# Feed-forward weight blocks whose odd rows lie 128 bytes further modulo 256, in a two-layer decoder step on one core

## The chip, the cores and the metric

The kernel runs on one core of a Trainium2 chip. The metric is the device time of one execution in microseconds, median of several runs; lower is better.

## What is computed

The reference runs two layers over 1,056 tokens (1,024 of a prompt, 32 of eight sampled sequences). Every layer is a mixing part (four token mixers behind one input projection) and a feed-forward part; the change touches only what is here called the channel part, which begins with the output projection:

```python
def finish(x, m, w_o, g_post_mix, g_pre_ffn, g_post_ffn, w_gate, w_up, w_down):
    x = x + rmsnorm(m @ w_o, g_post_mix)
    h = rmsnorm(x, g_pre_ffn)
    f = (jax.nn.silu(h @ w_gate) * (h @ w_up)) @ w_down
    return x + rmsnorm(f, g_post_ffn)
```

D_MODEL is 1024 and D_FF is 2816. Everything is float32 and has to keep float32's accuracy.

## The kernel before

**Three matmuls for one.** The kernel uses the type float32r, which keeps fewer bits. Each weight block and each activation is held as two tensors, a rounded one (`hi`) and the remainder (`lo`). The helper `terms` (its matmuls are recorded at L2199) issues for each product `hi x lo`, `hi x hi` and `lo x hi` (weight first), all into one PSUM bank. Each of the three loads its own 128x128 weights and moves 352 columns.

**Layout of the moving operands.** The T = 1056 tokens are taken in thirds (`th` = 0, 1, 2) of TH = 352. `act_hi` and `act_lo` are [128, 8, 1056] in float32: the row of block k starts 4,224 k bytes behind the start, and the third th 1,408 th bytes further. 4,224 is 16.5 times 256 and 1,408 is 5.5 times 256, so each odd k and th = 1 put the start of the moving operand 128 bytes further modulo 256. The gated activations `a_hi[i]` and `a_lo[i]` lie in places of 4,224 bytes (L2078 to L2086), and in the channel's order one of the pair of an i lies at the one half of 256 bytes and the other at the other half.

**Layout of the weights.** A weight block is 1024 rows by 128 columns, held as [128, 8, 128]: row block k starts 512 k bytes behind the start, so all eight start alike modulo 256. A place (`at_slot`, L2068) has 8,192 bytes, 4,096 for `w_hi` and 4,096 in which `w_raw` lands and `w_lo` replaces it. There are seven places: 0 to 2 go round, 3 to 5 serve the last blocks only, 6 serves block 3. Places 0 to 5 stand alike modulo 256, and alike with k even and th = 0 of the moving operands; place 6 stands 128 bytes off.

**The work of the channel part,** in the order that is written out by hand for TensorE (PE):

- the output projection: for th = 0 eight k's, in each eight output blocks d times three matmuls (24 matmuls on one moving row k); for th = 1 and 2 eight d's, in each eight k's times three. Its weights `wo_hi` and `wo_lo` stand alike modulo 256 for all k and d.
- 60 blocks j (`seq`, L2116) of three thirds, 24 matmuls to a third: 44 gate and up blocks, in parts of 8, 8 and 6 hidden blocks, and after each of the first two parts 8 down blocks, whose moving operands are `a_lo[k]`, `a_hi[k]`, `a_hi[k]`. A gate or up third is eight k's of `act_lo[k]`, `act_hi[k]`, `act_hi[k]`.
- the last six weight blocks (down, `sources[NB + k]`), for th = 0 k by k with eight d's in each, then th = 1 and 2 d by d.

**The supply of weights.** SP (the DMA queue) issues one 512 KB transfer to a block: `load(j)` (L2149, recorded at L2150) waits until the block that used the place is finished, three blocks earlier. ScalarE (ACT) rounds it (`split_w`, recorded at L2413), GpSimd (POOL) takes the remainder (`rest_of_w`, recorded at L2573), and PE waits for POOL's count (`w_lo_done`). VectorE (DVE) and ACT empty the PSUM banks. Nothing but the placement and the transfers of these blocks is changed.

```python
            def load(j):
                sp.dma_start(w_raw[slot(j)][:, 0:sources[j].shape[1], :], sources[j]).then_inc(w_in[slot(j)], 16)
            def terms(b, hi, lo, x_hi, x_lo, first, end):
                for i, (w, x) in enumerate(((hi, x_lo), (hi, x_hi), (lo, x_hi))):
                    ins = pe.matmul(bank(b), w, x, start=first and i == 0, stop=end and i == 2)
                return ins
```

Of the kernel before, what the change touches and what calls it, by code (L numbers as in the profile page):

```python
# [6 lines left out]
ALU = mybir.AluOpType  # L7
ACT = mybir.ActivationFunctionType
AX = mybir.AxisListType
F32 = mybir.dt.float32  # L10
BF16 = mybir.dt.bfloat16
I32 = mybir.dt.int32
F32R = mybir.dt.float32r


P = 128
# [23 lines left out]
KC = D // P  # L40
# [4 lines left out]
T = SEQ + NS  # L45
TH = T // 3
# [25 lines left out]
PAGES_AT = 170720  # L72
EARLY_END = PAGES_AT + 4 * (KIN + 2 * KC * GW + P + NS + P + NS + 4 * len(SLOTS))
# [331 lines left out]
def early_buffers(c, sem):  # L405
# [21 lines left out]
    c.rstd_y, c.rstd_x = (c.nc.alloc_sbuf_tensor_at(n, [P, TH], F32, offset=c.m_at + 24576 + 4 * TH * i) for n, i in (("rstd_y", 3), ("rstd_x", 4)))  # L427
    c.left_part = c.nc.alloc_sbuf_tensor_at("left_part", [P, TH], F32, offset=c.m_at + 24576 + 20 * TH)
# [1609 lines left out]
def channel(c, st):  # L2038
# [8 lines left out]
    def place(name, at, shape, dt=F32):  # L2047
        assert at + 4 * int(np.prod(shape[1:])) <= SBUF_END
        return nc.alloc_sbuf_tensor_at(name + c.tag, shape, dt, offset=at)
# [7 lines left out]
    y_even, y_even2 = place("y_even", c.m_at + 24576, [P, 6, TH]), place("y_even2", at_scr, [P, 2, TH])  # L2057
# [9 lines left out]

    at_slot = [c.m_at + 8192 * s_ for s_ in range(3)] + [rest + 8192 * s_ for s_ in range(3)] + [PAGES_AT]  # L2068
    w_hi = [place(f"w_hi{s_}", a, [P, KC, P], F32R) for s_, a in enumerate(at_slot)]
    w_raw = [place(f"w_raw{s_}", a + 4096, [P, KC, P]) for s_, a in enumerate(at_slot)]  # L2070
    w_lo = [place(f"w_lo{s_}", a + 4096, [P, KC, P], F32R) for s_, a in enumerate(at_slot)]
    sg_first, sg_next = place("silu_first", PAGES_AT + 8 * T, [P, 2, T]), place("silu", c.m_at + 24576, [P, 2, T])
# [11 lines left out]
    sq2, acc2 = place("down_sq", c.m_at + 24576, [P, 2, TH]), place("down_acc", c.m_at + 24576 + 8 * TH, [P, TH])  # L2084
# [61 lines left out]
    with nc.Block() as block:  # L2146
        @block.sync
        def _(sp):
            def load(j):  # L2149
                sp.dma_start(w_raw[slot(j)][:, 0:sources[j].shape[1], :], sources[j]).then_inc(w_in[slot(j)], 16)  # L2150
# [45 lines left out]
        def _(pe):  # L2196
# [58 lines left out]
            for n, (j, th) in enumerate(seq):  # L2255
# [13 lines left out]
                for k in range(K):  # L2269
                    if j == 0:  # L2270
                        pe.wait_ge(h_lo, KC * th + k + 1)
                    if what == "down" and i == 0:
                        pe.wait_ge(a_lo_done, up_nth[chunk(p_, k), th])
                    x_hi, x_lo = (a_hi[k][:, of(th)], a_lo[k][:, of(th)]) if what == "down" else (act_hi[:, k, of(th)], act_lo[:, k, of(th)])
                    ins = terms(unit_bank(n), w_hi[slot(j)][:, k, :], w_lo[slot(j)][:, k, :], x_hi, x_lo, k == 0, k == K - 1)
# [7 lines left out]
            def down(d, k, th):  # L2283
                j = NB + k
                return terms(down_bank(th, d), w_hi[slot(j)][:, d, :], w_lo[slot(j)][:, d, :], a_hi[k][:, of(th)], a_lo[k][:, of(th)], k == 0, k == NL - 1)
# [91 lines left out]
        def _(act):  # L2377
# [32 lines left out]
            def split_w(j):  # L2410
                K = sources[j].shape[1]
                act.wait_ge(w_in[slot(j)], 16 * (loads_before(j) + 1))
                act.activation(w_hi[slot(j)][:, 0:K, :], w_raw[slot(j)][:, 0:K, :], ACT.Copy).then_inc(w_hi_done, 1)  # L2413

# [140 lines left out]
        def _(pool):  # L2555
# [14 lines left out]
            def rest_of_w(j):  # L2570
                K = sources[j].shape[1]
                pool.wait_ge(w_hi_done, j + 1)
                pool.tensor_tensor(w_lo[slot(j)][:, 0:K, :], w_raw[slot(j)][:, 0:K, :], w_hi[slot(j)][:, 0:K, :].bitcast(F32), ALU.subtract).then_inc(w_lo_done, 1)  # L2573

# [208 lines left out]
```

## Time and profile before

| | us |
|---|---|
| median of 3 runs | 3132.66 (3129.66 to 3135.19) |
| the profiled execution's own time | 3102.04 |
| its span, first to last instruction | 3100.3 |
| mean granted TensorE clock | 0.991 |
| PE busy | 3011.1 (97%) |
| POOL busy | 734.4 (24%) |
| ACT busy | 1053.9 (34%) |
| DVE busy | 1434.6 (46%) |

The profile is one execution, and its rows add up to its own span, not to the median. "Busy" of PE is the union of overlapping matmuls: a matmul's own duration (about 320 ns) is twice the distance from its start to the next one's start, so what a matmul costs in a dense stretch is read from starts, or from a stretch's length over its count of matmuls. PEld is the loading of weights, which runs beside the matmuls. The channel part of layer 0 lies from about 680 to 1,530 us, that of layer 1 from about 2,210 us to the end.

### The profile page before, as it was taken

To read this page: it belongs to the slowest core of one execution; us is meant where nothing else is said; L and a number is where in the kernel's file an instruction comes from. 1 tells how busy PE (TensorE), PEld (TensorE's weight loads), DVE (VectorE), ACT (ScalarE), POOL (GpSimd) and SP (SyncE) were. 2 spreads that over 40 slices of the span, in tenths; PEclk is the share of its full clock that TensorE was granted. 3 is DMA by queue.
4 is the path that set the end of the run, shared out by engine and by line. 5 is a ranking of instruction groups with operands and counts; after the bars stand their busy time and mean duration, and the time that the engine had idled before them with its cause. 6 is when DMAs were issued, how large, how long until landed. Compare 5 with 4: busy or idle time off the path is not lost. (4 is left out here: it accounts for less than half of the span.)

```text
span 3100.3 us, 48849 instructions
## 1 busy us (share of the span) xinstructions
PE 3011.1 (97%) x19766; PEld 2644.6 (85%) x19766; DVE 1434.6 (46%) x3278; ACT 1053.9 (34%) x2094; POOL 734.4 (24%) x526
## 2 busy tenths in 40 slices
PE   8999999989999999999999999899999999999998
PEld 6777766669999999999977777665799999999997
DVE  5579675557611111122565887565574111111125
ACT  4376535554311111011333665355542111110112
POOL 3002041324312122243300201313352122121131
PEclk9999999999999999999999999999999999999999
DMA  5120235651211111121321111456411111111131
GB/s 181 37 64 28 70 150 172 226 204 49 71 44 48 48 47 43 48 66 59 113 79 45 47 35 50 181 184 228 169 58 60 48 48 42 48 48 48 41 118 56
DMA packets 254071, 263.54 MB, mean 85 GB/s; under 512 B 24993, under 2 KB 224570, under 8 KB 253850
## 3 DMA queue, kind: packets, MB, share of 16 engines
q1 hardware_dynamic: 233370, 189.11, 19.5%
q0 software_dynamic: 20480, 71.32, 6.6%
q8 instruction: 159, 2.61, 0.3%
q14 instruction: 62, 0.51, 0.1%
HBM read 229.73 MB, written 30.65 MB: 84 GB/s over the span
## 5 line engine op out<-in xcount | busy, mean ns | idle before, releaser
L2199 PE MATMUL ps<-act_lo,w_hi 128*128 128x352 f32 x2112 | 684.2, 324 | 5.0 <-DVE act_lo L2651 3.1
L2199 PE MATMUL ps<-act_hi,w_hi 128*128 128x352 f32 x2112 | 677.9, 321 | 0.0
L2199 PE MATMUL ps<-act_hi,w_lo 128*128 128x352 f32 x2112 | 677.2, 321 | 0.0
L2573 POOL TENSOR_TENSOR w_lo<-w_raw,w_hi 128x1024 fp32r<-128x1024 f32 x132 | 322.0, 2441 | 1022.9 <-ACT w_hi L2413 1022.8
L709 PE MATMUL ps<-w_in_slots,hT 128*128 128x256 f32 (+1 forms) x2048 | 448.5, 375 | 3.4 <-PEq L192 3.4
L709 PEld LDWEIGHTS ps<-w_in_slots,hT 128*128 128x128 f32 x2048 | 374.7, 193 | 58.6 <-issue 12.4
L2199 PEld LDWEIGHTS ps<-act_lo,w_hi 128*128 128x128 f32 x2112 | 396.7, 188 | 10.2 <-issue 5.2
L2664 DVE TENSOR_TENSOR a_raw<-ps,silu 128x352 f32<-128x352 f32 x120 | 63.0, 525 | 728.7 <-PE ps L2199 728.7
L2199 PEld LDWEIGHTS ps<-act_hi,w_hi 128*128 128x128 f32 x2112 | 397.4, 188 | 0.2
L2199 PEld LDWEIGHTS ps<-act_hi,w_lo 128*128 128x128 f32 x2112 | 396.5, 188 | 0.0
L2199 PE MATMUL ps<-a_lo,w_hi 128*128 128x352 f32 x1056 | 344.1, 326 | 0.0
L2199 PE MATMUL ps<-a_hi,w_lo 128*128 128x352 f32 x1056 | 339.9, 322 | 0.0
L2199 PE MATMUL ps<-a_hi,w_hi 128*128 128x352 f32 x1056 | 339.7, 322 | 0.0
L2413 ACT ACTIVATE w_hi<-w_raw 128x1024 fp32r<-128x1024 f32 x132 | 139.7, 1058 | 460.5 <-DMA w_raw<-in_w_down 286.8
L2461 ACT ACTIVATE silu<-ps 128x352 f32<-128x352 f32 x120 | 55.7, 464 | 674.0 <-PE ps L2199 674.0
L712 PE MATMUL ps<-hT,w_in_slots 128*128 128x352 f32 x768 | 229.7, 460 | 0.0
L1157 DVE TENSOR_SCALAR_CACHE_REDUCE mask_c<-score,sel_cand 128x1024 bf16<-128x1024 f32 x248 | 219.2, 939 | 0.4
L712 PEld LDWEIGHTS ps<-hT,w_in_slots 128*128 128x128 f32 x768 | 145.2, 190 | 80.8 <-issue 1.6
L2199 PEld LDWEIGHTS ps<-a_lo,w_hi 128*128 128x128 f32 x1056 | 199.4, 189 | 1.1
L2199 PEld LDWEIGHTS ps<-a_hi,w_hi 128*128 128x128 f32 x1056 | 198.3, 188 | 1.1
L2199 PEld LDWEIGHTS ps<-a_hi,w_lo 128*128 128x128 f32 x1056 | 198.1, 188 | 0.0
L940 ACT ACTIVATE mask_s<-xT,sel_cand 32x2080 bf16<-32x2080 f32 x62 | 125.2, 2020 | 32.9 <-DVE sel_cand L1162 32.6
(368 smaller groups left out, 4255.2 us busy)
## 6 DMA issues: line engine op xcount, KB each, us to landing
w_raw<-in_w_gate SPq DMA_DIRECT2D x44, 512.0 KB, 3.8
w_raw<-in_w_up SPq DMA_DIRECT2D x44, 512.0 KB, 3.8
w_raw<-in_w_down SPq DMA_DIRECT2D x44, 512.0 KB, 3.8
w_in_slots<-in_w_in SPq DMA_DIRECT2D x18, 1024.0 KB, 5.3
xpark<-xT SPq DMA_DIRECT2D x9, 1408.0 KB, 5.7
xT<-xpark SPq DMA_DIRECT2D x6, 1408.0 KB, 15.5
hT<-xpark SPq DMA_DIRECT2D x6, 1408.0 KB, 12.8
wo_raw<-in_w_o SPq DMA_DIRECT2D x16, 512.0 KB, 5.2
```

What stands on the lines that cost most here:

```text
L709: ins = pe.matmul(ps[:m, bank[i], 0:w], hT[:, k, cols(n)], W[:, g % 2, k, 0:w], start=(k == 0), stop=(k == KC - 1))
L712: ins = pe.matmul(ps[:, bank[i], 0:TH], W[:, g % 2, k, n * P:(n + 1) * P], hT[:, k, th * TH:(th + 1) * TH], start=(k == 0), stop=(k == KC ...
L940: act.activation(junk[x], score[x], ACT.Sign, bias=cand[:rows[x], at[x]].bitcast(F32), accum_out=count[:rows[x], at[x]]).then_inc(q["count ...
L1157: return dve.tensor_scalar(junk[x], score[x], value, None, ALU.is_ge, ALU.add, accum_out=acc)
L2199: ins = pe.matmul(bank(b), w, x, start=first and i == 0, stop=end and i == 2)
L2413: act.activation(w_hi[slot(j)][:, 0:K, :], w_raw[slot(j)][:, 0:K, :], ACT.Copy).then_inc(w_hi_done, 1)
L2461: act.activation(sg(f, th), bank(unit_bank(n)), ACT.Silu).then_inc(sg_done, 1)
L2573: pool.tensor_tensor(w_lo[slot(j)][:, 0:K, :], w_raw[slot(j)][:, 0:K, :], w_hi[slot(j)][:, 0:K, :].bitcast(F32), ALU.subtract).then_inc(w_ ...
L2664: dve.tensor_tensor(raw, bank(unit_bank(n)), sg(chunk(p_, i), th), ALU.mult).then_inc(mul, 1)
```

## The change

Each weight tensor becomes [128, 2, 512] with a distance of 4,224 bytes between its two halves: the first holds the row blocks of even k, the second those of odd k (`at_row`). `w_hi` and `w_raw`/`w_lo` are interleaved, 2,048 bytes apart, so a place is 8,320 bytes long instead of 8,192. The start of a row block of odd k is now 128 bytes off that of even k modulo 256. As 8,320 is 32.5 times 256, places 1 and 4 are also shifted by 128 bytes as a whole. `load` issues two transfers of 256 KB, one to a half (even and odd row blocks; for the last six weight blocks even and odd d), and ACT waits for both. ACT and POOL work on [128, 2, 512] instead of [128, 8, 128] with the same 1,024 elements to a partition. What stood behind the three places (`y_even`, `silu`, `down_sq`, `rstd_y` and others) moves by 384 bytes. The order of the matmuls, their counts and their operands are unchanged.

```diff
--- before.py
+++ after.py
@@ -70,6 +70,8 @@
 
 KIN = PAST // 512 * DB * P
 PAGES_AT = 170720
+W_SLOT = 8320
+PAST_SLOTS = 3 * W_SLOT
 EARLY_END = PAGES_AT + 4 * (KIN + 2 * KC * GW + P + NS + P + NS + 4 * len(SLOTS))
 GAINS_AT = 228704
 SBUF_END = 229344
@@ -424,8 +426,8 @@
     c.early_sems = [*c.w_in, *c.ki_sem, c.const_in, c.x_parked, c.x_last_parked]
 
     c.gains = c.nc.alloc_sbuf_tensor_at("gains", [P, 4, KC], F32, offset=GAINS_AT)
-    c.rstd_y, c.rstd_x = (c.nc.alloc_sbuf_tensor_at(n, [P, TH], F32, offset=c.m_at + 24576 + 4 * TH * i) for n, i in (("rstd_y", 3), ("rstd_x", 4)))
-    c.left_part = c.nc.alloc_sbuf_tensor_at("left_part", [P, TH], F32, offset=c.m_at + 24576 + 20 * TH)
+    c.rstd_y, c.rstd_x = (c.nc.alloc_sbuf_tensor_at(n, [P, TH], F32, offset=c.m_at + PAST_SLOTS + 4 * TH * i) for n, i in (("rstd_y", 3), ("rstd_x", 4)))
+    c.left_part = c.nc.alloc_sbuf_tensor_at("left_part", [P, TH], F32, offset=c.m_at + PAST_SLOTS + 20 * TH)
     c.first_root = c.nc.alloc_sbuf_tensor_at("first_root", [P, 3 * P], F32, offset=ROOT_AT)
     c.wo_raw = c.nc.alloc_sbuf_tensor_at("wo_raw", [P, KC, D], F32, offset=c.m_at + 8 * KC * T + 4 * KC * D)
     c.wo_hi = c.nc.alloc_sbuf_tensor_at("wo_hi", [P, KC, D], F32R, offset=c.m_at + 8 * KC * T)
@@ -2054,7 +2056,7 @@
     over = rest + 4 * KC * T
     wo_hi, wo_raw, wo_lo = c.wo_hi, c.wo_raw, c.wo_lo
     at_scr = over + 8 * KC * D
-    y_even, y_even2 = place("y_even", c.m_at + 24576, [P, 6, TH]), place("y_even2", at_scr, [P, 2, TH])
+    y_even, y_even2 = place("y_even", c.m_at + PAST_SLOTS, [P, 6, TH]), place("y_even2", at_scr, [P, 2, TH])
     y_odd = place("y_odd", c.m_at + 13312, [P, KC, TH])
     sq, acc, rstd = place("mix_sq", at_scr + 8 * TH, [P, 2, TH]), place("mix_acc", at_scr + 16 * TH, [P, TH]), place("mix_rstd", at_scr + 20 * TH, [P, TH])
     gains = c.gains
@@ -2065,11 +2067,16 @@
 
 
 
-    at_slot = [c.m_at + 8192 * s_ for s_ in range(3)] + [rest + 8192 * s_ for s_ in range(3)] + [PAGES_AT]
-    w_hi = [place(f"w_hi{s_}", a, [P, KC, P], F32R) for s_, a in enumerate(at_slot)]
-    w_raw = [place(f"w_raw{s_}", a + 4096, [P, KC, P]) for s_, a in enumerate(at_slot)]
-    w_lo = [place(f"w_lo{s_}", a + 4096, [P, KC, P], F32R) for s_, a in enumerate(at_slot)]
-    sg_first, sg_next = place("silu_first", PAGES_AT + 8 * T, [P, 2, T]), place("silu", c.m_at + 24576, [P, 2, T])
+    at_slot = [c.m_at + W_SLOT * s_ for s_ in range(3)] + [rest + W_SLOT * s_ for s_ in range(3)] + [PAGES_AT]
+    w_hi = [place(f"w_hi{s_}", a, [P, 2, T], F32R)[:, :, 0:4 * P] for s_, a in enumerate(at_slot)]
+    w_raw = [place(f"w_raw{s_}", a + 2048, [P, 2, T])[:, :, 0:4 * P] for s_, a in enumerate(at_slot)]
+    w_lo = [place(f"w_lo{s_}", a + 2048, [P, 2, T], F32R)[:, :, 0:4 * P] for s_, a in enumerate(at_slot)]
+    assert W_SLOT >= 4 * T + 4096
+
+    def at_row(w, k):
+        return w[:, k % 2, k // 2 * P:(k // 2 + 1) * P]
+
+    sg_first, sg_next = place("silu_first", PAGES_AT + 8 * T, [P, 2, T]), place("silu", c.m_at + PAST_SLOTS, [P, 2, T])
 
     def sg(f, th):
         return (sg_first if f < 2 else sg_next)[:, f % 2, of(th)]
@@ -2081,7 +2088,7 @@
     a_lo = [place(f"a_lo{i}", at_tile[2 * i + 1], [P, T], F32R) for i in range(KC)]
     a_raw = place("a_raw", over + 12 * T, [P, 2, TH])
     assert over + 12 * T + 8 * TH <= PAGES_AT and max(at_tile) + 4 * T <= GAINS_AT
-    sq2, acc2 = place("down_sq", c.m_at + 24576, [P, 2, TH]), place("down_acc", c.m_at + 24576 + 8 * TH, [P, TH])
+    sq2, acc2 = place("down_sq", c.m_at + PAST_SLOTS, [P, 2, TH]), place("down_acc", c.m_at + PAST_SLOTS + 8 * TH, [P, TH])
     rstd1, rstd2 = c.rstd_y, c.rstd_x
 
 
@@ -2147,7 +2154,8 @@
         @block.sync
         def _(sp):
             def load(j):
-                sp.dma_start(w_raw[slot(j)][:, 0:sources[j].shape[1], :], sources[j]).then_inc(w_in[slot(j)], 16)
+                for b in range(2):
+                    sp.dma_start(w_raw[slot(j)][:, b, :].rearrange("p (a n) -> p a n", a=4), sources[j][:, b::2, :]).then_inc(w_in[slot(j)], 16)
 
             for k in range(2, KC):
                 load_output_rows(c, sp, k)
@@ -2272,7 +2280,7 @@
                     if what == "down" and i == 0:
                         pe.wait_ge(a_lo_done, up_nth[chunk(p_, k), th])
                     x_hi, x_lo = (a_hi[k][:, of(th)], a_lo[k][:, of(th)]) if what == "down" else (act_hi[:, k, of(th)], act_lo[:, k, of(th)])
-                    ins = terms(unit_bank(n), w_hi[slot(j)][:, k, :], w_lo[slot(j)][:, k, :], x_hi, x_lo, k == 0, k == K - 1)
+                    ins = terms(unit_bank(n), at_row(w_hi[slot(j)], k), at_row(w_lo[slot(j)], k), x_hi, x_lo, k == 0, k == K - 1)
                 ins.then_inc(mm, 1)
                 if n == 1:
                     mix_sum_1(2)
@@ -2282,7 +2290,7 @@
 
             def down(d, k, th):
                 j = NB + k
-                return terms(down_bank(th, d), w_hi[slot(j)][:, d, :], w_lo[slot(j)][:, d, :], a_hi[k][:, of(th)], a_lo[k][:, of(th)], k == 0, k == NL - 1)
+                return terms(down_bank(th, d), at_row(w_hi[slot(j)], d), at_row(w_lo[slot(j)], d), a_hi[k][:, of(th)], a_lo[k][:, of(th)], k == 0, k == NL - 1)
 
             def sum_y(th):
                 pe.wait_ge(d_add, (KC - 1) * (th + 1))
@@ -2408,9 +2416,8 @@
                     act.activation(act_hi[:, k, of(th)], y(th, k), ACT.Copy).then_inc(h_hi, 1)
 
             def split_w(j):
-                K = sources[j].shape[1]
-                act.wait_ge(w_in[slot(j)], 16 * (loads_before(j) + 1))
-                act.activation(w_hi[slot(j)][:, 0:K, :], w_raw[slot(j)][:, 0:K, :], ACT.Copy).then_inc(w_hi_done, 1)
+                act.wait_ge(w_in[slot(j)], 32 * (loads_before(j) + 1))
+                act.activation(w_hi[slot(j)], w_raw[slot(j)], ACT.Copy).then_inc(w_hi_done, 1)
 
             for k in range(2, KC):
                 act.wait_ge(wo_in[k], 16)
@@ -2568,9 +2575,8 @@
                     pool.tensor_tensor(y(th, 0), y(th, 0), y(th, k), ALU.add).then_inc(x_add, 1)
 
             def rest_of_w(j):
-                K = sources[j].shape[1]
                 pool.wait_ge(w_hi_done, j + 1)
-                pool.tensor_tensor(w_lo[slot(j)][:, 0:K, :], w_raw[slot(j)][:, 0:K, :], w_hi[slot(j)][:, 0:K, :].bitcast(F32), ALU.subtract).then_inc(w_lo_done, 1)
+                pool.tensor_tensor(w_lo[slot(j)], w_raw[slot(j)], w_hi[slot(j)].bitcast(F32), ALU.subtract).then_inc(w_lo_done, 1)
 
             for k in range(2, KC):
                 pool.wait_ge(wo_hi_done, k - 1)
```

## Rows read from the trace of the kernel before

**Rows 1.** The page: span, busy time, share of the span and instructions of each engine.
```profile
span 3100.3 us, 48849 instructions
...
PE 3011.1 (97%) x19766; PEld 2644.6 (85%) x19766; DVE 1434.6 (46%) x3278; ACT 1053.9 (34%) x2094; POOL 734.4 (24%) x526
```

**Rows 2.** A stretch of layer 1: us, PE busy (matmuls), granted clock, DMA share, GB/s.
```profile
2343.20:3021.40 678.20, 678.20 (x4246) 1.00 0.18 55
```

**Rows 3.** The page's groups of matmuls, all recorded at L2199.
```profile
L2199 PE MATMUL ps<-act_lo,w_hi 128*128 128x352 f32 x2112 | 684.2, 324 | 5.0 <-DVE act_lo L2651 3.1
...
L2199 PE MATMUL ps<-a_lo,w_hi 128*128 128x352 f32 x1056 | 344.1, 326 | 0.0
```

**Rows 4.** Timeline of SP, second half of layer 1: start us, us, engine line op out<-in.
```profile
2566.20 0.37 SPq L2150 DMA_DIRECT2D w_raw<-in_w_gate  x1
...
2589.24 0.37 SPq L2150 DMA_DIRECT2D w_raw<-in_w_gate  x1
2600.69 0.37 SPq L2150 DMA_DIRECT2D w_raw<-in_w_up  x1
...
2657.92 0.37 SPq L2150 DMA_DIRECT2D w_raw<-in_w_gate  x1
```

**Rows 5.** Timeline of PE, output projection of layer 1, first third.
```profile
2234.49 0.32 PE L2199 MATMUL ps<-act_lo,wo_hi 128*128 128x352 f32 x1
...
2238.33 0.32 PE L2199 MATMUL ps<-act_lo,wo_hi 128*128 128x352 f32 x1
...
2242.13 0.32 PE L2199 MATMUL ps<-act_lo,wo_hi 128*128 128x352 f32 x1
```

**Rows 6.** Timeline of PE, output projection: layer 1 second and last third, layer 0 last third.
```profile
2254.21 0.33 PE L2199 MATMUL ps<-act_lo,wo_hi 128*128 128x352 f32 x1
...
2258.07 0.33 PE L2199 MATMUL ps<-act_lo,wo_hi 128*128 128x352 f32 x1
...
2287.22 0.32 PE L2199 MATMUL ps<-act_lo,wo_hi 128*128 128x352 f32 x1
...
2291.03 0.32 PE L2199 MATMUL ps<-act_lo,wo_hi 128*128 128x352 f32 x1
...
754.88 0.32 PE L2199 MATMUL ps<-act_lo,wo_hi 128*128 128x352 f32 x1
...
758.73 0.32 PE L2199 MATMUL ps<-act_lo,wo_hi 128*128 128x352 f32 x1
```

**Rows 7.** Timeline of PE and of its weight load in one gate block.
```profile
2600.02 0.32 PE L2199 MATMUL ps<-act_lo,w_hi 128*128 128x352 f32 x1
...
2600.02 0.19 PEld L2199 LDWEIGHTS ps<-act_hi,w_hi 128*128 128x128 f32 x1
```

**Rows 8.** The answer for the tile w_raw: split, remainder, and transfers to landing.
```profile
L2413 ACT ACTIVATE w_hi<-w_raw x132: 1052/1060/1068, 738.6 to 3009.3; 128x1024 fp32r<-128x1024 f32 x132
L2573 POOL TENSOR_TENSOR w_lo<-w_raw,w_hi x132: 2365/2394/2774, 739.7 to 3013.6; 128x1024 fp32r<-128x1024 f32 x132
...
DMA to landing us min/median/max: 3.3/3.8/6.1
```

**Rows 9.** Timelines of SP, ACT, POOL and PE at the last six blocks of layer 1.
```profile
3001.91 1.75 SPq L2150 DMA_DIRECT2D w_raw<-in_w_down  x4
...
3005.43 1.06 ACT L2413 ACTIVATE w_hi<-w_raw 128x1024 fp32r<-128x1024 f32 x1 [10.46 <-DMA w_raw<-in_w_down]
...
3006.57 9.48 POOL L2573 TENSOR_TENSOR w_lo<-w_raw,w_hi 128x1024 fp32r<-128x1024 f32 x4 [9.11 <-ACT w_hi L2413]
...
3009.39 0.32 PE L2199 MATMUL ps<-a_lo,w_hi 128*128 128x352 f32 x1
```

**Rows 10.** Timelines of SP, ACT and PE where layer 1 starts its second weight block.
```profile
2307.82 0.37 SPq L2150 DMA_DIRECT2D w_raw<-in_w_up  x1
...
2312.91 1.06 ACT L2413 ACTIVATE w_hi<-w_raw 128x1024 fp32r<-128x1024 f32 x1
...
2316.56 0.40 PE L2199 MATMUL ps<-act_lo,w_hi 128*128 128x352 f32 x1 [0.90 <-POOL w_lo L2573]
```

## The prediction, made before the changed kernel was run

> **What bounds the kernel now.** First the page: TensorE is busy for 3011.1 of 3100.3 us, and no other engine for half of the span [rows 1]. Then a stretch of the channel part of layer 1: PE works through 678.20 us without a pause, at a granted clock of 1.00 [rows 2]. There the time is the number of matmuls times the distance from one start to the next, 678.20 / 4246 = 159.7 ns. The change touches the weights of 3 x 2112 matmuls in gate and up blocks and 3 x 1056 in down blocks [rows 3], 6336 + 3168 = 9504 in all. One nanosecond of distance is 9.5 us, or 0.3% of the run. So everything hangs on whether the place of the weights alters the distance.
>
> It does differ between stretches with the same shapes. SP's loads are released by the end of a block, so their distances are PE's pace. The last two down blocks take 2589.24 - 2566.20 = 23.04 us for 144 matmuls, 160.0 ns each. The five gate and up blocks behind them take 2657.92 - 2600.69 = 57.23 us for 360, 159.0 ns each [rows 4]. In the output projection a k of 24 matmuls takes 3.84 us, the next k only 3.80 us, 160.0 against 158.3 ns, and between these two nothing changes but the half of 256 bytes in which the moving row starts [rows 5]. I read from this that the distance depends on how the moving row stands to the weights that are loaded beside it.
>
> Which weights are these? The load for the next matmul starts as the current one starts, both at 2600.02 [rows 7]. So I compare each moving row with the weights of the matmul behind it: "same" (S) where both start in the same half of 256 bytes, "other" (O) where not. The trace doesn't prove this pairing. Block 3 alone has other weights, too few to settle it.
>
> **The change, part by part.**
>
> *Gate and up, 6336 matmuls.* Before, a third runs SSS OOO SSS OOO, as the row's half changes with k and the weights stay: 159.0 ns. After, the weights change with k too. The first two matmuls of a k load weights of the same k, the third those of the next, so it runs SSO SSO, or in th = 1 and in places 1 and 4 OOS OOS. Nothing in the trace has this in a gate block, but the down blocks of before do: their `a_lo` and `a_hi` lie in different halves, and for most of a third they run OSS OSS or SOO SOO, the same cycles. They take 160.0 ns [rows 4]. So I expect 1.0 ns more: 6336 x 1.0 = 6.3 us longer.
>
> *Down, 3168 matmuls.* Their rows change half within k and now the weights change with k: in most places that makes strict alternation, OSOS. No stretch of before shows it. The nearest rows from below are the fast k's of the output projection, 158.3 ns [rows 5]; from above its second third, 24 matmuls in 2258.07 - 2254.21 = 3.86 us, 160.9 ns [rows 6]. That is 1.7 ns less to 0.9 ns more than the 160.0 of now, -5.4 to +2.9 us. I take 159.7, about the middle and the mean of the long stretch [rows 2]: 3168 x -0.3 = -1.0 us.
>
> *Two transfers instead of one.* SP issues 264 for 132. In the middle of the part the supply has slack: a load comes three blocks of 11.45 us ahead, and needs 3.8 us to landing, 1.06 on ACT and 2.39 on POOL [rows 8]. A second issue is 0.37 us. It costs nothing; without this cover each block would pay about half a microsecond. Two places are tight. Where the second block of a layer is loaded, the transfer is issued at 2307.82, and ACT takes it at 2312.91, without a wait for it; landed at 2307.82 + 3.8 = 2311.6 it has 1.3 us left, more than the second issue [rows 10]. At the end, ACT waits for the third of the last six blocks until 3005.43, POOL has its remainder at 3006.57 + 9.48 / 4 = 3008.94, and PE starts on it at 3009.39, only 0.45 us later [rows 9]. There the transfers have run in 4 KB pieces from a contiguous row of `w_down` and are now cut to 512 bytes each; the shortest landing of all, 3.3 us, and the median of 3.8 [rows 8] bound that at 0.5 us, and the second issue adds up to 0.4. So PE waits 0 to 0.5 us at this point of each layer: I take 0.25, twice, 0.5 us. The other three have a pace of 2.37 us on POOL against 3.84 on PE and stay hidden. The copies of `xpark` behind them come some 2 us later, and none is needed before the first third of these blocks ends, some 15 us after PE's start on the third block (four times 24 matmuls).
>
> *ACT and POOL on two runs of 512 elements* instead of one of 1,024: 0, within 0.1 us of either instruction, hidden behind the same 11.45 us, except in the chain just told, where it lies within the 0.25. *The 384 bytes by which `y_even`, `silu` and others move:* 0; they are read by engines that wait for PE.
>
> **Sum:** 6.3 - 1.0 + 0.5 = +5.8 us on the profiled execution's 3102.0. The median of the runs, 3132.7, is 30.6 us above that execution, and I add the difference to it: 3138.5 us. I can't tell under 0.2%, 6.3 us, from no change, so this lies on the border. With the bounds of the down blocks and of the wait, the forecast's own range is +1 to +10 us, 3133 to 3143.
>
> **The rule that speaks against any effect.** The distance does vary with the half, 160.0 against 158.3 ns in neighbouring k's [rows 5]. Against that, the Trainium skill, TensorE: Matmul & The Clock Gate, section "Step by step: what each phase is for", says that the two read ports are independent and that loading the next weights takes no read bandwidth from the running matmul, and its page SBUF — State Buffer, section "Who interferes with whom", that PE never waits on anyone. By that rule the sum would be +0.5 us; by the rows it is +5.8 us. The trace doesn't agree with it in rows 5.
>
> **The rivals.**
>
> 1. *No effect (12%).* The pace would be set by the moving row alone, as the halves of the rows don't change: 3132.7 + 0.5 = 3133 us. For it: in all rows the weights stood still, so I have seen only the row move. Against it: nothing explains then why a row that starts 128 bytes later runs faster. This is also the case in which the change is made but reaches nothing.
>
> 2. *Faster: a steady pairing (25%).* Perhaps the half of the weights that meet a row is that of its own k, because the reads lag behind the starts that the trace shows. Then each gate and up third is now in one relation throughout, all S or all O, as the k's of the output projection are: 158.3 ns in one and 160.0 in the other [rows 5]. Thirds and places share these about evenly, 159.15 on average, which would be no gain. It decides for a gain if both relations, now without any switch of half between k's, settle at the faster figure: 9504 x (159.35 - 158.3) = 10 us less, 3123 us. (159.35 is the mean over both kinds of block, (6336 x 159.0 + 3168 x 160.0) / 9504.) The place is the whole run of blocks; the point from which it shows is a mean under 158.7 ns. If the collisions went altogether, more would come; no row prices that.
>
> 3. *Clearly slower: the bad cycle (13%).* The pace isn't fixed by the sequence of halves alone. The last third of the output projection has the same addresses in both layers, and 24 matmuls take 3.81 us in layer 1 but 3.85 in layer 0, and the second third 3.86 [rows 6]. So there is more than one steady cycle, and gate blocks now are in a good one. If the new pattern locks into that of 160.9 ns: 9504 x 1.55 = 15 us, 3148 us.
>
> **How the numbers follow.** The forecast has 50%, the rivals 12, 25 and 13. Of the forecast, 20 lie within 0.2% and 30 above; with the rivals that makes 0.25 faster, 0.32 the same, 0.43 slower. The predicted time is the forecast's, rounded to 3138. The range of 3117 to 3149 takes in the faster rival with something below it, and the slower one's price; what is left out is mostly a gain larger than any row prices.
>
> **What would show it.** PE's pace by SP's distances: 11.52 us for a gate or up block where it is 11.45 now, and the last down blocks between 11.40 and 11.58 (now 11.52). The third of the last six blocks should have PE waiting for POOL by up to 0.5 us. Loads should land in about 4.2 us, with no wait of PE elsewhere. If gate and up blocks take 11.45 us again, the pairing plays no part; under 11.42, my pairing is the wrong one or the collisions are really gone. A wait of ACT that reaches PE in mid-stream would make the whole account of the transfers wrong.

## The result, and the profile after

| | before | after |
|---|---|---|
| median, 15 runs each | 3133.51 us | 3140.74 us |
| ratio to before, 95% interval | | 1.0027 (1.0020 to 1.0035) |
| the same against before, kernel run again | 3129.95 us | 3142.66 us, 1.0035 (1.0022 to 1.0049) |
| the profiled execution's own time, its span | 3102.04, 3100.3 us | 3140.74, 3138.9 us |
| a gate or up block (5 blocks / 5) | 11.446 us | 11.546 us |
| a gate or up matmul | 159.0 ns | 160.4 ns |
| a down matmul | 160.0 ns | 160.2 ns |

The kernel became slower by 0.27%, 8.5 us by the ratio (6.3 to 11.0). One of the 15 runs of the changed kernel took 6065.44 us and is not counted in the ratio; the medians alone lie 7.2 us apart. The page after, its span and engines, which answer to [rows 1]:

```profile
span 3138.9 us, 48981 instructions
...
PE 3034.1 (97%) x19766; PEld 2655.8 (85%) x19766; DVE 1427.6 (45%) x3278; ACT 1054.4 (34%) x2094; POOL 734.8 (23%) x526
```

The 38.6 us between the two profiled spans are not what the change costs. Before's own median moves from one comparison to the next: 3103 us on the chip that ran most experiments below, 3130 us on another, 3134 us here. The profile of before (3102 us) fits the first, that of after the others. In the first 700 us, which the change doesn't touch, the granted clock was 0.99 in the one and 0.97 in the other. So the two traces may be compared only where PE's pace is read within one stretch at one clock. These are SP's load issues of after in layer 1, in the columns of [rows 4]; `x2` is now a pair of transfers:

```profile
2417.04 0.92 SPq L2158 DMA_DIRECT2D w_raw<-in_w_gate  x2
...
2601.75 0.92 SPq L2158 DMA_DIRECT2D w_raw<-in_w_gate  x2
...
2624.82 0.92 SPq L2158 DMA_DIRECT2D w_raw<-in_w_gate  x2
2636.39 0.92 SPq L2158 DMA_DIRECT2D w_raw<-in_w_up  x2
...
2694.12 0.92 SPq L2158 DMA_DIRECT2D w_raw<-in_w_gate  x2
...
3005.86 0.92 SPq L2158 DMA_DIRECT2D w_raw<-in_w_up  x2
```

And two of before, the issues at the same points of the work as the first and the last of these:

```profile
2382.62 0.37 SPq L2150 DMA_DIRECT2D w_raw<-in_w_gate  x1
...
2967.57 0.37 SPq L2150 DMA_DIRECT2D w_raw<-in_w_up  x1
```

The five gate and up blocks of after in a view by window: us, PE busy (matmuls), granted clock, DMA share, GB/s.

```profile
2636.39:2694.12 57.73, 57.73 (x362) 1.00 0.16 46
```

The clock is 1.00 there, as in [rows 2], and PE never pauses.

Between the first and the last lie 51 blocks of 72 matmuls. Before they take 2967.57 - 2382.62 = 584.95 us, 159.3 ns a matmul; after 3005.86 - 2417.04 = 588.82 us, 160.35 ns. That is 1.05 ns on 9504 matmuls, 10 us. The starts of these matmuls, from the first to the last of each layer, say the same: 783.37 + 776.84 us after, 778.37 + 771.89 before, 9.95 us more. The timing's 8.5 us (6.3 to 11.0) has room for all of it. By kind: the two down blocks take 2624.82 - 2601.75 = 23.07 us (23.04 before), the five gate and up blocks 2694.12 - 2636.39 = 57.73 us (57.23 before). The loss is nearly all in the gate and up blocks.

It isn't spread evenly over them. ACT's first operation after the end of a third is released by PE, so its starts show when the thirds th = 0, 1, 2 of a block end. Two blocks of after, the first in place 1, the second in place 0 (in brackets ACT's wait and who ended it):

```profile
2651.79 0.47 ACT L2468 ACTIVATE silu<-ps 128x352 f32<-128x352 f32 x1 [10.36 <-PE ps L2207]
2655.65 0.47 ACT L2468 ACTIVATE silu<-ps 128x352 f32<-128x352 f32 x1 [3.40 <-PE ps L2207]
2659.48 0.47 ACT L2468 ACTIVATE silu<-ps 128x352 f32<-128x352 f32 x1 [3.36 <-PE ps L2207]
...
2674.91 0.47 ACT L2468 ACTIVATE silu<-ps 128x352 f32<-128x352 f32 x1 [10.47 <-PE ps L2207]
2678.74 0.47 ACT L2468 ACTIVATE silu<-ps 128x352 f32<-128x352 f32 x1 [3.36 <-PE ps L2207]
2682.61 0.47 ACT L2468 ACTIVATE silu<-ps 128x352 f32<-128x352 f32 x1 [3.40 <-PE ps L2207]
```

In place 1 the third th = 1 takes 2655.65 - 2651.79 = 3.86 us and th = 2 takes 3.83; in place 0 it is the other way round, 3.83 and 3.87. Place 1 stands 128 bytes off place 0, and so does th = 1 off th = 2. From the trace's starts in nanoseconds: where the moving row and the weights of its own k start in the same half of 256 bytes, the gaps between starts repeat as 162, 160, 163, 162, 158, 162 ns, each give or take 1, and whole thirds have a mean of 161.0 to 161.1. Where they start in different halves, the gaps settle after up to half of the third at 161, 161, 155 ns, mean 159; with the less regular matmuls ahead of that, whole thirds have 159.4 to 160.0.

The loads, to compare with [rows 8]: operations on the tile `w_raw` with duration in ns min/median/max.

```profile
L2420 ACT ACTIVATE w_hi<-w_raw x132: 1048/1061/1067, 755.4 to 3051.3; 128x1024 fp32r<-128x1024 f32 x132
L2579 POOL TENSOR_TENSOR w_lo<-w_raw,w_hi x132: 2358/2400/2755, 756.5 to 3053.6; 128x1024 fp32r<-128x1024 f32 x132
...
DMA to landing us min/median/max: 3.9/4.4/5.5
```

ACT and POOL work as long as before, and a pair of transfers holds SP for 0.92 us where it was 0.37. The landing, 4.4 us at the median against 3.8 [rows 8], may not be put down to the change: only 8 of the 264 transfers have one in this trace, and on the chip of 3130 us the kernel's single transfers land later, too. The same line of two kernels below, first the two transfers alone on the chip of 3103 us, then the shift of 128 bytes, with one transfer to a block, on that of 3130 us:

```profile
DMA to landing us min/median/max: 2.9/3.3/5.6
...
DMA to landing us min/median/max: 4.5/5.3/6.1
```

On the first chip both transfers of a pair are there 3.86 us after the first is issued (median of 131 pairs), where one of 512 KB takes 3.81. The 5.3 us rest on four transfers.

The third of the last six blocks of layer 1, to compare with [rows 9]: ACT's split of it, POOL's remainder, PE's last matmul before it and first on it, and the weight load of that one.

```profile
3044.65 1.06 ACT L2420 ACTIVATE w_hi<-w_raw 128x1024 fp32r<-128x1024 f32 x1 [10.56 <-DMA w_raw<-in_w_down]
...
3045.79 2.40 POOL L2579 TENSOR_TENSOR w_lo<-w_raw,w_hi 128x1024 fp32r<-128x1024 f32 x1 [9.23 <-ACT w_hi L2420]
...
3047.85 0.32 PE L2207 MATMUL ps<-a_hi,w_lo 128*128 128x352 f32 x1
3048.24 0.43 PE L2207 MATMUL ps<-a_lo,w_hi 128*128 128x352 f32 x1
...
3048.24 0.19 PEld L2207 LDWEIGHTS ps<-a_lo,w_hi 128*128 128x128 f32 x1 [0.36 <-POOL w_lo L2579]
```

ACT gets the block at 3044.65, POOL ends at 3045.79 + 2.40 = 3048.19, and the weight load behind it has waited 0.36 us for that. PE starts 0.39 us after the matmul before, where 0.16 is the pace, and this matmul lasts 0.43 instead of 0.32: together 0.34 us are lost.

Where the second block begins, to compare with [rows 10]: SP's issue, ACT's split, PE's start.

```profile
2341.92 0.93 SPq L2158 DMA_DIRECT2D w_raw<-in_w_up  x2
...
2347.00 1.06 ACT L2420 ACTIVATE w_hi<-w_raw 128x1024 fp32r<-128x1024 f32 x1
...
2350.64 0.40 PE L2207 MATMUL ps<-act_lo,w_hi 128*128 128x352 f32 x1 [0.81 <-POOL w_lo L2579]
```

ACT takes the tile without a wait for its transfers, and PE's wait for POOL is 0.81 us (0.90 before).

### The profile page after: what moved, and what is told of

The parts are those of the page before. It is cut to its first block and busy times, and to the rows that moved or that the text cites. A ratio compares the mean times of both kernels' runs of the same rounds, so it can differ in the third digit from the quotient of the medians.

```text
span 3138.9 us, 48981 instructions
## 1 busy us (share of the span) xinstructions
PE 3034.1 (97%) x19766; PEld 2655.8 (85%) x19766; DVE 1427.6 (45%) x3278; ACT 1054.4 (34%) x2094; POOL 734.8 (23%) x526
```

## The experiments

Eleven kernels were run, each timed against the kernel before on the same chip. In the stretches compared, the granted clock was 1.00 in every trace. Pace is read as above, from SP's issues around the same five gate and up blocks (360 matmuls). "Own k" means that a moving row is compared with the weights of its own k, "next matmul" with those of the matmul behind it, as the forecast had it.

### The two transfers alone

The kernel before with its layout, each load cut into even and odd row blocks.

```diff
             def load(j):
-                sp.dma_start(w_raw[slot(j)][:, 0:sources[j].shape[1], :], sources[j]).then_inc(w_in[slot(j)], 16)
+                for h in range(2):
+                    sp.dma_start(w_raw[slot(j)][:, h::2, :], sources[j][:, h::2, :]).then_inc(w_in[slot(j)], 16)
...
-                act.wait_ge(w_in[slot(j)], 16 * (loads_before(j) + 1))
+                act.wait_ge(w_in[slot(j)], 32 * (loads_before(j) + 1))
```

> The old placement (all row blocks alike modulo 256), but each block loaded in two transfers of 256 KB. Theory (the pace follows the placement, the transfers cost only at the end of a layer): gate and up blocks 11.45 us apart and down blocks 11.52 us apart as before; PE waits for POOL's remainder of the third of the last six blocks, 0.2 to 0.4 us in each layer; in total 0.4 to 0.8 us over the kernel before, which timing can't tell from nothing (ratio 1.000). Rival (the 4.4 us that each layer's blocks gained come from the transfers, through later weights or busier queues): blocks at 11.53 us again, ratio near 1.0025.

Measured: 3105.77 against 3103.02 us, ratio 1.0004 (0.9995 to 1.0013). SP's issues around the five blocks, and the weight load of PE at the third of the last six blocks:

```profile
2605.28 0.92 SPq L2151 DMA_DIRECT2D w_raw<-in_w_up  x2
...
2662.51 0.92 SPq L2151 DMA_DIRECT2D w_raw<-in_w_gate  x2
...
3014.43 0.19 PEld L2200 LDWEIGHTS ps<-a_lo,w_hi 128*128 128x128 f32 x1 [0.57 <-POOL w_lo L2574]
```

The five blocks take 57.23 us, exactly before's. The one thing that moves is PE's wait, 0.57 us here and 0.36 in layer 0, which the kernel before doesn't have. The transfers cost some 0.5 us a layer at that place and nothing elsewhere. The converse, the new layout with one transfer to a block, was not tried.

### The longer places alone

The blocks as before, but with 8,320 bytes from place to place.

```diff
-    at_slot = [c.m_at + 8192 * s_ for s_ in range(3)] + [rest + 8192 * s_ for s_ in range(3)] + [PAGES_AT]
+    at_slot = [c.m_at + 8320 * s_ for s_ in range(3)] + [rest + 8320 * s_ for s_ in range(3)] + [PAGES_AT]
```

(and 24,960 for 24,576 where `y_even` and what follows begin)

> The old blocks and one transfer each, only with places of 8,320 bytes, so that places 1 and 4 as a whole stand 128 bytes off. Theory (row block against row block decides, and a third still runs through k's in the same relation and k's in the other one by turns): gate and up 11.45 us, ratio 1.000. Rival (the length of the places, or what moved behind them, slows the kernel): 11.5 us or more in all blocks, ratio 1.002 or more.

Measured: 3106.58 against 3103.02 us, 1.0007 (0.9998 to 1.0016).

```profile
2607.28 0.37 SPq L2150 DMA_DIRECT2D w_raw<-in_w_up  x1
...
2664.55 0.37 SPq L2150 DMA_DIRECT2D w_raw<-in_w_gate  x1
```

57.27 us for the five blocks. A shift of whole places by 128 bytes, and the 384 bytes by which `y_even` and others move, cost nothing that the timing can tell. The trace has a little: over both layers, from the first to the last matmul of the weight blocks, 1.75 us more than before, 1.0 of them in gate and up thirds, where the mean is 159.14 ns for 158.99. With the 1.0 us that the same count gives for the two transfers alone, some 7 of the 9.95 us remain. They go with the new layout of a block: the weights of odd k lie 128 bytes off those of even k, and `w_hi` and `w_lo` are interleaved. No kernel had the second without the first.

### All places alike, in either half

The changed kernel with places of 8,448 bytes (33 times 256), so that all stand as place 0 does; and the same with all of them 128 bytes further, as place 1.

```diff
-W_SLOT = 8320
+W_SLOT = 8448
```
```diff
-    at_slot = [c.m_at + W_SLOT * s_ for s_ in range(3)] + [rest + W_SLOT * s_ for s_ in range(3)] + [PAGES_AT]
+    at_slot = [c.m_at + 128 + W_SLOT * s_ for s_ in range(3)] + [rest + 128 + W_SLOT * s_ for s_ in range(3)] + [PAGES_AT]
```

> The changed kernel with places of 8,448 bytes, 33 times 256, so that all places but the seventh stand alike. In the changed kernel's trace a gate or up third in which moving row and weights of the same k start in the same half of 256 bytes runs at 161.0 ns per matmul, and one in which they start in different halves settles at 159.0. Theory (that relation decides): now thirds 0 and 2 run at 161.0 and third 1 at 159.0 in every place, 2 of 3 slow instead of 5 of 9: mean 160.5 to 160.6 instead of 160.4, 11.56 us to a block, about 1 us more than the changed kernel, ratio 1.003. Rival (each place's own stretch of memory or the changes between places cost the time): the places all run like place 0 or better and the ratio falls to 1.001.

> As places_alike, with places 0 to 5 all moved by 128 bytes. Theory: the roles change, thirds 0 and 2 settle at 159.0 ns and third 1 runs at 161.0, 1 of 3 slow: mean 159.9 ns with the first matmuls of a third, 11.51 us to a block, some 4 us less than places_alike, ratio 1.0015 to 1.002. It decides against any theory in which the distance between blocks of odd and even k costs the time by itself: by that one this kernel is as slow as places_alike, ratio 1.003.

Measured: 3110.93 us, 1.0026 (1.0015 to 1.0036), and 3108.76 us, 1.0019 (1.0010 to 1.0028), both against 3103.02. First the places alike: SP around the five blocks, and the ends of the thirds of one block that lies in place 1.

```profile
2606.34 0.92 SPq L2158 DMA_DIRECT2D w_raw<-in_w_up  x2
...
2664.14 0.92 SPq L2158 DMA_DIRECT2D w_raw<-in_w_gate  x2
...
2621.77 0.46 ACT L2468 ACTIVATE silu<-ps 128x352 f32<-128x352 f32 x1 [10.38 <-PE ps L2207]
2625.60 0.46 ACT L2468 ACTIVATE silu<-ps 128x352 f32<-128x352 f32 x1 [3.37 <-PE ps L2207]
2629.46 0.46 ACT L2468 ACTIVATE silu<-ps 128x352 f32<-128x352 f32 x1 [3.40 <-PE ps L2207]
```

Then the places 128 bytes further, the same block:

```profile
2605.71 0.92 SPq L2158 DMA_DIRECT2D w_raw<-in_w_up  x2
...
2663.24 0.92 SPq L2158 DMA_DIRECT2D w_raw<-in_w_gate  x2
...
2621.03 0.46 ACT L2468 ACTIVATE silu<-ps 128x352 f32<-128x352 f32 x1 [10.39 <-PE ps L2207]
2624.90 0.46 ACT L2468 ACTIVATE silu<-ps 128x352 f32<-128x352 f32 x1 [3.40 <-PE ps L2207]
2628.72 0.47 ACT L2468 ACTIVATE silu<-ps 128x352 f32<-128x352 f32 x1 [3.37 <-PE ps L2207]
```

Alike, th = 1 takes 3.83 us and th = 2 takes 3.86; in the changed kernel the block in this place had 3.86 and 3.83. Shifted back by 128 bytes it has 3.87 and 3.82 again. Which thirds are slow therefore follows the half of the place and of th together, by own k: same half 161.0 to 161.3 ns over whole thirds, other half 158.8 to 160.0. With two slow thirds of three the five blocks take 57.80 us, with one 57.53, and the changed kernel, which mixes the places, lies between with 57.73. The timing alone doesn't part the two, as their intervals overlap; by the starts of the matmuls the second is 4.4 us quicker, as expected. By "next matmul" a shift by 128 bytes turns SSO into OOS, and all thirds would have kept one pace.

### The remainder alone 128 bytes further

The kernel before with `w_hi` where it was and `w_raw`/`w_lo` 128 bytes further, in places of 8,448 bytes.

```diff
-    w_raw = [place(f"w_raw{s_}", a + 4096, [P, KC, P]) for s_, a in enumerate(at_slot)]
-    w_lo = [place(f"w_lo{s_}", a + 4096, [P, KC, P], F32R) for s_, a in enumerate(at_slot)]
+    w_raw = [place(f"w_raw{s_}", a + 4224, [P, KC, P]) for s_, a in enumerate(at_slot)]
+    w_lo = [place(f"w_lo{s_}", a + 4224, [P, KC, P], F32R) for s_, a in enumerate(at_slot)]
```

> The old blocks and one transfer each, in places of 8,448 bytes that all stand alike, but w_lo (and w_raw) 128 bytes off w_hi modulo 256. So the weights change half twice in every k, at the third matmul and back. The runs so far: a third in one relation all through runs at 161.0 (same half) or 159.0 ns (other half) where weights and rows change half with every k, at 160.0 or 158.3 in the output projection where neither does, and at 159.0 where only the rows do. Theory A (relation of row and own weights, plus about 0.85 ns a matmul, 2.5 ns a change, for a change of half of the weights): mean 159.15 + 2 x 0.85 = 160.8 ns in gate and up, 11.58 us to a block, ratio 1.003 to 1.004. Theory B (the relation alone, half of the matmuls in either): 159.1 to 159.3, 11.46 us, ratio 1.000 to 1.001.

Measured: 3109.17 against 3103.28 us, 1.0017 (1.0008 to 1.0027).

```profile
2604.46 0.37 SPq L2150 DMA_DIRECT2D w_raw<-in_w_up  x1
...
2661.92 0.37 SPq L2150 DMA_DIRECT2D w_raw<-in_w_gate  x1
```

57.46 us, 159.6 ns, with thirds of 158.9, 159.7 and 160.3 ns; down blocks 160.8. This meets neither of the figures that were set against each other. What the moving rows of a k meet within three matmuls matters, but no rule that I had gives the size.

### The whole weights shifted by 64, 32, 96 and 128 bytes

The kernel before, all seven places shifted by one constant; nothing else but the start of `y_even` and what follows.

```diff
-    at_slot = [c.m_at + 8192 * s_ for s_ in range(3)] + [rest + 8192 * s_ for s_ in range(3)] + [PAGES_AT]
+    at_slot = [c.m_at + 64 + 8192 * s_ for s_ in range(3)] + [rest + 64 + 8192 * s_ for s_ in range(3)] + [PAGES_AT + 64]
```

> The old kernel with all weight places 64 bytes further. If the memory is divided into two halves of 256 bytes, a distance of 64 (or 192) bytes is neither the same nor the other half: gate and up between 158.3 and 161.0 ns, about 159.5, ratio 1.000 to 1.003, and third 1 as third 0. If the division is finer than 128 bytes and collisions are what the distance contains above the shortest ones seen, 155 ns, moving all weights by 64 bytes may take them out of the way: 157 ns or less, 11.3 us to a block, ratio 0.995 or less. If only 128 matters and not where in it a block starts, 159.0 and ratio 1.000.

> The same with 32 bytes. As for 64: about 159 to 160 ns and a ratio within 0.2% of 1 if the halves of 256 bytes are what counts; another value than with 64, in either direction and by more than 0.5 ns, if a finer division does.

> The old kernel with all weight places 96 bytes further; 0, 64 and 32 bytes gave 159.0, 160.2 and 162.0 ns in gate and up. If only the distance of the two starts counts, whichever is ahead, 96 is as far from 128 as 32 is from 0 and costs as much: 162 ns, ratio 1.007. If who is ahead counts, another value: between 159 and 161, ratio 1.000 to 1.004. A gain (below 158.5 ns) would beat both kernels; I give that 1 in 5.

> The old kernel with all weight places 128 bytes further. In a gate or up third same and other half only trade places: 159.0 ns, 11.45 us, ratio within 0.1% of 1. If the half in which weights lie counts by itself: another pace in all thirds, 160 ns or 158.

| shift | median, before's | ratio (95%) | gate, up ns | down ns |
|---|---|---|---|---|
| 32 bytes | 3126.22, 3103.28 | 1.0070 (1.0056 to 1.0084) | 162.0 | 161.8 |
| 64 bytes | 3115.58, 3103.28 | 1.0037 (1.0024 to 1.0051) | 160.2 | 160.8 |
| 96 bytes | 3138.59, 3129.95 | 1.0021 (1.0012 to 1.0031) | 160.0 | 160.0 |
| 128 bytes | 3132.29, 3129.95 | 1.0003 (0.9994 to 1.0013) | 159.0 | 160.0 |

The issues around the five blocks, with the shift of 32 bytes:

```profile
2619.21 0.37 SPq L2150 DMA_DIRECT2D w_raw<-in_w_up  x1
...
2677.54 0.37 SPq L2150 DMA_DIRECT2D w_raw<-in_w_gate  x1
```

and with that of 128 bytes:

```profile
2634.50 0.37 SPq L2150 DMA_DIRECT2D w_raw<-in_w_up  x1
...
2691.74 0.37 SPq L2150 DMA_DIRECT2D w_raw<-in_w_gate  x1
```

58.33 us against 57.24. Here no transfer, block, wait or order is changed, so where the weights start is worth up to 3.0 ns a matmul by itself, 0.7% of the run. The rows' own halves, which differ by k and th, are the same in all four. That disposes of rival 1. Whether their distance from the moving rows counts, or their own start, the shifts of 32, 64 and 96 bytes can't tell, as no kernel moved the rows by such an amount. The shift of 96 bytes at least goes against the distance alone, whichever is ahead: by that it would have cost as much as 32, and it cost 160.0 ns for 162.0.

A whole shift of 128 bytes turns every S into O and every O into S and changes the mean by nothing, since a gate or up third has as many of one as of the other. But single thirds of the down blocks trade places: th = 1 has 160.2 ns before and 159.8 shifted, th = 2 has 159.8 and 160.2. For 128 bytes it is thus the relation to the rows that counts and not the weights' own start.

### Rows by four instead of by two

The changed kernel with k = 0 to 3 in the first half and 4 to 7 in the second. By own k each third then has S and O in turn within its fours, as before the change.

```diff
     def at_row(w, k):
-        return w[:, k % 2, k // 2 * P:(k // 2 + 1) * P]
+        return w[:, k // 4, k % 4 * P:(k % 4 + 1) * P]
...
-                    sp.dma_start(w_raw[slot(j)][:, b, :].rearrange("p (a n) -> p a n", a=4), sources[j][:, b::2, :]).then_inc(w_in[slot(j)], 16)
+                    sp.dma_start(w_raw[slot(j)][:, b, :].rearrange("p (a n) -> p a n", a=4), sources[j][:, 4 * b:4 * b + 4, :]).then_inc(w_in[slot(j)], 16)
```

> The changed kernel with nothing altered but which row blocks lie in which half: 0 to 3 in the first, 4 to 7 in the second, instead of even and odd. Same places, same two runs of 512 elements, same two transfers. The weights now change half once in a third, not with every k, and moving row and weights are in the same and in different halves by turns, as before the change. Theory (relation row by row and its change with every k decide): gate and up back to 159.0 to 159.2 ns, 11.45 to 11.47 us, ratio 1.0003 to 1.001. Rival (the split tensors, the longer places or the two transfers slow the kernel): 11.53 us and 1.0027 again.

Measured: 3137.06 against 3129.95 us, 1.0019 (1.0009 to 1.0028), 159.9 ns in the gate and up blocks. The expectation missed. The ends of thirds, in place 1 and then in place 0:

```profile
2653.41 0.46 ACT L2468 ACTIVATE silu<-ps 128x352 f32<-128x352 f32 x1 [10.39 <-PE ps L2207]
2657.22 0.46 ACT L2468 ACTIVATE silu<-ps 128x352 f32<-128x352 f32 x1 [3.35 <-PE ps L2207]
2661.08 0.47 ACT L2468 ACTIVATE silu<-ps 128x352 f32<-128x352 f32 x1 [3.39 <-PE ps L2207]
...
2676.39 0.47 ACT L2468 ACTIVATE silu<-ps 128x352 f32<-128x352 f32 x1 [10.48 <-PE ps L2207]
2680.24 0.46 ACT L2468 ACTIVATE silu<-ps 128x352 f32<-128x352 f32 x1 [3.38 <-PE ps L2207]
2684.10 0.46 ACT L2468 ACTIVATE silu<-ps 128x352 f32<-128x352 f32 x1 [3.39 <-PE ps L2207]
```

In place 1, th = 1 takes 3.81 us and th = 2 takes 3.86; in place 0 they take 3.85 and 3.86. Single thirds lie anywhere from 158.8 to 161.1 ns, and the same place and third, with the same addresses, can have either: th = 2 in place 0 goes from 158.8 to 160.7. The sequence of relations by own k is that of before except for one turn in the middle of a third, and the pace is 0.9 ns longer. So own k names the slow thirds of the changed kernel, but isn't the law of the pace. The block, 11.52 us, is nearer to what the rival gave, 11.53: the split tensors, the longer places and the two transfers are all in this kernel, and so is a loss of 6.8 of the 9.95 us. Only a third of the loss went with the even and odd rows. How much of the rest the interleaved layout takes by itself, and how much the 128 bytes that still lie between the halves, is not told apart.

### The changed kernel again

> The changed kernel itself, beside the experiments. Both theories: ratio 1.0025 to 1.003, 11.53 us to a gate or up block, as in its first trace.

Measured: 3142.66 against 3129.95 us, 1.0035 (1.0022 to 1.0049). SP's issues around the five blocks are at 2640.20 and 2697.93, 57.73 us apart, and the two kinds of matmul take 160.4 and 160.2 ns, as in the first trace.

That the channel parts start later in the profile of after is not due to the change, as is seen in the matmuls of the output projection, whose first and last start stand behind the durations: first of the two transfers alone, on the chip with the median of 3103 us, then of the shift of 128 bytes, on that with 3130 us.

```profile
L2200 PE MATMUL ps<-act_lo,wo_hi x368: 318/322/590, 684.0 to 2311.4; 128*128 128x352 f32 x184
```

```profile
L2199 PE MATMUL ps<-act_lo,wo_hi x368: 318/322/593, 703.0 to 2340.3; 128*128 128x352 f32 x184
```

Both have the code of before up to there, and one comes to its first output projection 19.0 us later than the other. The last start lies 2340.3 - 2311.4 = 28.9 us apart, that is, another 9.9 us further. Of the 19.0 us, 13.7 come between 360 and 620 us, and there the granted clock differs: by 100 us from 400 to 700, it is 0.97, 1.00 and 0.95 in the first trace and 0.95, 0.96 and 0.93 in the second. That the clock accounts for all of it is not shown, nor what lowers it.

## Why the prediction was right, and where not

The forecast was 3138 us, 0.2% above the median shown then, with a range of 3117 to 3149; 3140.74 us was measured. The case that happened is the forecast's own, slower by 1 to 10 us, and not by a wait but by the pace of PE. Point by point:

- *What bounds the kernel.* Right. In the five blocks PE never paused, and the whole loss but 0.8 us is a longer distance between starts.
- *The distance depends on how the moving row stands to the weights.* Right, and now shown: in the trace of before only rows moved; with the weights moved as a whole, all else as it was, it goes from 159.0 to 162.0 ns. **The rule** of the Trainium skill, TensorE: Matmul & The Clock Gate, section "Step-by-step: what each phase is for" (two independent read ports, loading the next weights takes no read bandwidth from the running matmul), with SBUF — State Buffer, section "Who interferes with whom" (PE never waits on anyone), gave +0.5 us. The runs don't bear out that the weights' side leaves the pace alone: 12 us for a shift of 64 bytes and 23 for one of 32. The second section is about other engines; no run here tests that.
- *Which weights: those of the matmul behind.* Wrong, or at least not what names the slow thirds. By it all thirds should have kept one pace; the trace has thirds of 161.1 and of 159.4 to 160.0 ns, and they follow the row's own k.
- *Gate and up, + 1.0 ns x 6336 = 6.3 us.* The term that was mis-sized. It measured + 1.4 ns, 6336 x 1.4 = 8.9 us. The step that failed is the transfer of the down blocks' 160.0 ns because "the same cycles" run there. The gate blocks went into a cycle of 161.1 in five of nine combinations of place and third, and had 159.4 to 160.0 in the others. The mean is near the forecast's since it lies between, not since the cycle was the right one: that the total came out so close is luck in part.
- *Down, - 0.3 ns x 3168 = -1.0 us.* Wrong in sign, within its bounds: + 0.16 ns, 3168 x 0.16 = 0.5 us. By thirds it goes from 159.5 to 160.7 ns. The quick pace of 158.3 ns showed nowhere.
- *Two transfers, 0.25 us twice.* Right in place and mechanism, at the upper part of its bounds: 0.36 us of waiting in the changed kernel, 0.36 and 0.57 in the transfers alone; about 0.4 us twice. Nothing elsewhere, as said. The landing in "about 4.2 us" was too dear: on the chip of before's profile a single one of the two takes 3.3 us and the pair 3.86 (3.81 before).
- *The sum.* 8.9 + 0.5 + 0.8 = 10.2 us by the trace where 5.8 was forecast; 8.5 (6.3 to 11.0) by the timing.
- *The 30.6 us between the profiled execution and the median.* Adding them was right. They belong to the chip or the execution and not to the change, as before's own medians of 3103 and 3130 us show; an engineer who had compared the two spans would have found 38.6 us.
- *Rival 1, no effect,* fell with the shifts of 32 to 96 bytes. *Rival 2, a steady pairing by own k,* was half right: thirds do settle in one relation throughout, but at 161.1 and 159 ns, not at 160.0 and 158.3 as in the output projection, so that no gain comes of it. *Rival 3, the bad cycle,* is near what slow thirds have, 161.1 for the 160.9 that it named, but only in about half of them.

Shown, then, is that the place of the weights alone sets the pace, and that the change lengthened it; not shown is how much of it the 128 bytes between odd and even k did and how much the rest of the new layout, as no kernel had the one without the other. What stays open is the law itself. No rule tried gives the cycles: own k fails on the rows by four, neither theory fits the shifted remainder, and 32 bytes cost more than 64. The division that matters is finer than 128 bytes. Shifts of 16 bytes weren't tried. None of the eleven kernels was faster than the one before.

## What to carry to other kernels

Where a kernel is bound by back-to-back matmuls with a weight load each, the start of the weights against the start of the moving row is worth measuring: here 0.7% lay between placements that differ in 32 bytes. Try it as a plain shift of a whole tensor first, since that costs no code and no transfers, and read the pace in one stretch rather than the total. A pace that was seen with one sequence of addresses shouldn't be carried to another, even if the sequence of halves looks alike; give such a term the whole span between the paces that the trace holds.

## What was not expected of the hardware

- The dependence is fine and not monotonic: weights 32, 64, 96 and 128 bytes further give 162.0, 160.2, 160.0 and 159.0 ns a gate or up matmul; 159.0 without a shift, too.
- In the changed kernel, the pace takes repeating cycles that fit neither one matmul nor one k: six gaps of 162, 160, 163, 162, 158, 162 ns, or three of 161, 161, 155.
- Two chips differ by some 27 us on the same kernel (3103 and 3130 us). Of this, 19 us are there before the first output projection, while the five gate and up blocks take the same on both (57.23 us with the two transfers alone, 57.24 with the shift of 128 bytes). Where the 19 us arise, the granted clock of the one is lower, and its single transfers land after 5.3 us instead of 3.8. Each chip ran at its own time, so chip and time are not told apart.
- Two 256 KB issues at once keep SP for 0.92 us, more than twice 0.37, but on the same chip both have landed 3.86 us after the first issue, no later than one of 512 KB (3.81).
